# Twelve weight slots for the experts instead of six, and the upper and lower output rows of narrow experts in one tile

## What is computed

```python
combine = jnp.einsum('tk,tke->te', w, jax.nn.one_hot(eidx, N_EXPERTS, dtype=jnp.float32))
hid = jax.nn.silu(jnp.einsum('td,edf->tef', t, w_gate)) * jnp.einsum('td,edf->tef', t, w_up)
hid = hid * combine.astype(hid.dtype)[..., None]
return jnp.einsum('tef,efd->td', hid, w_down).reshape(B, L, D)
```

## Time and profile before

| | us |
|---|---|
| median of 3 runs | 1324.78 |
| lowest and highest | 1319.63, 1330.17 |
| the profiled execution | 1327.07 |
| its span, first to last instruction | 1325.4 |
| PE busy in the span | 1187.1 (90%) |
| DVE, ACT busy | 702.0 (53%), 433.7 (33%) |
| chain that ended last, its shares | PE 69%, DMA 15%, DVE 8% |
| expert stage of layer 0 | 379.2 to 645 |
| expert stage of layer 1 | 1018.0 to 1289 |

### The profile page before, as it was taken

The page is one execution under the profiler, slowest core; times in us unless marked ns, Lnnn a source line. Parts: engine busy times, 40 slices in busy tenths (PEclk is TensorE's granted clock), DMA queues, the critical chain, the costliest instruction groups (busy, mean ns, idle before and its releaser), DMA issues.

```text
span 1325.4 us, 20656 instructions
## 1 busy us (share of the span) xinstructions
PE 1187.1 (90%) x6340; PEld 755.7 (57%) x6341; DVE 702.0 (53%) x1425; ACT 433.7 (33%) x771; POOL 9.8 (1%) x30
## 2 busy tenths in 40 slices
PE   5999999998579999999689999999958899999973
PEld 2796555588354455444369755557926454455443
DVE  4365877664722344444566387767464234244445
ACT  2425555442331122222152345544233222122213
POOL 1000000000000000000000000000000000000000
PEclk8899999999699999999799999999978999999996
DMA  8743655423146899999783265552320889889961
GB/s 312 227 130 123 227 190 177 142 66 127 38 158 228 317 387 422 422 421 422 273 285 108 87 221 182 174 187 66 127 69 27 307 348 423 322 320 423 422 260 48
DMA packets 101983, 305.36 MB, mean 230 GB/s; under 512 B 7136, under 2 KB 47824, under 8 KB 77328
## 3 DMA queue, kind: packets, MB, share of 16 engines
q1 hardware_dynamic: 99248, 301.62, 61.0%
q10 hardware_dynamic: 2528, 2.50, 0.6%
q0 software_dynamic: 128, 0.26, 0.1%
HBM read 302.53 MB, written 1.84 MB: 230 GB/s over the span
## 4 chain that ended last, share of the span: by engine, by line
PE 69%; DMA 15%; DVE 8%; issue 4%; ACT 4%; DVEq 0%; SPq 0%; ACTq 0%
PE ps L694 14%; DMA ring<-in_w_e_up 13%; PE ps L557 9%; PE ps L589 6%; PE ps L560 6%; PE ps L680 5%; PE ps L715 4%; PE ps L716 3%; PE ps L717 3%; PE ps L612 3%; PE ps L878 3%; PE ps L641 2%; PE ps L653 2%; PE ps L785 2%; PE ps L760 1%
## 5 line engine op out<-in xcount | busy, mean ns | idle before, releaser
L557 PE MATMUL ps<-ring,xgT 128*64 128x256 f32 x1728 | 205.7, 387 | 16.5 <-issue 10.6
L557 PEld LDWEIGHTS ps<-ring,xgT 128*64 128x64 f32 x1728 | 125.9, 138 | 103.1 <-issue 27.7
L1420 DVE SCALAR_TENSOR_TENSOR nat<-ps,qT,nat 128x512 f32<-128x512 f32 x192 | 132.8, 745 | 80.6 <-PE ps L612 80.6
L694 PE MATMUL ps<-hT,ring 128*128 128x384 f32 x512 | 173.4, 492 | 0.0
L589 PE MATMUL ps<-ring,conv 128*64 128x512 f32 (+1 forms) x512 | 134.2, 597 | 7.2 <-issue 4.1
L1527 DVE SCALAR_TENSOR_TENSOR conv<-ub,dw,conv 128x414 f32<-128x414 f32 x240 | 136.6, 644 | 0.0
L694 PEld LDWEIGHTS ps<-hT,ring 128*128 128x128 f32 x512 | 95.4, 191 | 66.4 <-issue 7.2
L1411 DVE TENSOR_TENSOR orow_lo<-ps,orow_hi 64x512 fp32r<-64x512 f32 (+1 forms) x64 | 44.1, 689 | 112.5 <-ACT orow_hi L1037 111.7
L589 PEld LDWEIGHTS ps<-ring,conv 128*64 128x64 f32 (+1 forms) x512 | 48.3, 145 | 78.5 <-issue 78.2
L1402 DVE TENSOR_TENSOR csq<-csq,ps 128x256 f32<-128x256 f32 (+1 forms) x32 | 14.8, 463 | 129.4 <-PE ps L557 83.8
L560 PE MATMUL ps<-ring,xgT 128*128 128x512 f32 x160 | 74.8, 624 | 8.4 <-issue 8.4
(11 more groups left out here) (254 smaller groups left out, 1797.3 us busy)
## 6 DMA issues: line engine op xcount, KB each, us to landing
ring<-in_w_e_gate SPq DMA_DIRECT2D x64, 1024.0 KB, 10.1
ring<-in_w_e_up SPq DMA_DIRECT2D x64, 1024.0 KB, 10.8
ring<-in_w_e_down SPq DMA_DIRECT2D x64, 1024.0 KB, 9.8
ring<-in_w_ada SPq DMA_DIRECT2D x48, 1024.0 KB, 7.7
ring<-in_w_in SPq DMA_DIRECT2D x30, 1024.0 KB, 6.1
ring<-in_w_out SPq DMA_DIRECT2D x8, 1024.0 KB, 5.9
ring<-in_w_attn_proj SPq DMA_DIRECT2D x4, 1024.0 KB, 5.6
ring<-in_w_conv_proj SPq DMA_DIRECT2D x4, 1024.0 KB, 6.6
```

Source lines behind the costliest of these rows:

```text
L557: last = pe.matmul(ps[64 * hh:64 * hh + 64, b, 0:256], xgT[:, k, 0:64], ring[s][:, o + hh * 256:o + (hh + 1) * 256], start=(k == 0), stop= ...
L694: last = pe.matmul(ps[:, b, 0:T], ring[c % SLOTS][:, o:o + P], rhs(k), start=(k == 0), stop=(k == k_tiles - 1))
L1420: dve.scalar_tensor_tensor(sums, ps[:, b, :], weight[:, t, bass.ds(at, 1)], sums, ALU.mult, ALU.add).then_inc(fr[b], 1)
```

## The change

- Six more slots of 1 MB, `odd0` to `odd5`, lie over tiles that the experts don't need (`sig` and what follows it, `probs`, `hT`, `qkv`). Experts with an even number use `ring`, those with an odd number `odd`; the semaphores are `landed` and `landed_odd`. `hid`, `silu`, `hidT`, `own` and `xgT` move to other places.
- Expert 1's loads are issued between expert 0's, each once its place is free: the slots over `probs` and `sig` during the mixer's output stage, the one after the second norm, the last two (down) when `spread` is done. From expert 2 on, a slot waits for the expert two ahead.
- PE's program now has the first expert, the second expert (four branches) and a loop over pairs, whose body has two experts of four branches each. Counted in the program's order, with a float32 matmul as its four records, the first expert is about 330 instructions in both; the loop body was about 815, the second expert is about 775, and the new loop body about 1,580.
- A narrow expert's remainders go to the other 64 partitions of `orow_hi`, so `back` has two matmuls of 128 rows for each token tile instead of four of 64. Wide experts are as before.
- The counts of the start (`START`) grow from 3 to 8, with the waits that refer to them.

```diff
-SLOT_USES = (NCHUNKS + MOE_CHUNKS * NE) // SLOTS
+SLOT_USES = NCHUNKS // SLOTS + NE // 2
...
-START = 3
+START = 8
...
-        hid = flat(csq, 0, DE)
-        silu = flat(csq, DE, 2 * DE)
-        hidT = flat(conv, 0, DE).rearrange("p (k n) -> p k n", k=KE)
-        own = flat(conv, DE, DE + NT * P).rearrange("p (t n) -> p t n", t=NT)
+        hid = over("hid", "qkv", 0, [P, DE], F32)
+        silu = over("silu", "qkv", DE, [P, DE], F32)
+        hidT = over("hidT", "qkv", 3 * D + NT * P, [P, KE, P], F32)
+        own = over("own", "hT", NT * ROWS, [P, NT, P], F32)
...
-        xgT = over("xgT", "probs", 0, [P, KD, P], F32)
+        xgT = over("xgT", "qT", 2 * NT * BLOCKS * NE, [P, KD, P], F32)
+        assert start_of["kT"] >= start_of["qT"] + 4 * (2 * NT * BLOCKS * NE + KD * P)
+
+
+        odd = [over("odd0", "sig", 0, [P, SLOT], F32), over("odd1", "sig", SLOT, [P, SLOT], F32),
+               over("odd2", "probs", 0, [P, SLOT], F32), over("odd3", "probs", SLOT, [P, SLOT], F32),
+               over("odd4", "hT", 0, [P, SLOT], F32), over("odd5", "qkv", 3 * D + NT * P + DE, [P, SLOT], F32)]
...
+        landed_odd = [sem(f"landed_odd{s}") for s in range(SLOTS)]
...
-                for j in range(MOE_CHUNKS):
+                    load(ring[s], landed[s], src)
+
+                def first_even(j):
                     wait_chunk_used(NCHUNKS - SLOTS + j, l)
-                    load(j, landed[j], expert_chunk(j, l * NE))
-
-                def reload(e, first=False):
+                    load(ring[j], landed[j], expert_chunk(j, l * NE))
+
+                def first_odd(j):
+                    if j == 2:
+                        b, n = use("pv", UNITS - 1, l)
+                        sp.wait_ge(full[b], n + 1)
+                    elif j < 2:
+                        b, n = use("cproj", KD - 1, l)
+                        sp.wait_ge(full[b], n + 1)
+                    elif j == 3:
+                        sp.wait_ge(xn_r, l * (2 * KD) + 2 * KD)
+                    else:
+                        b, n = use("spread", 2 * KD - 1, l)
+                        sp.wait_ge(full[b], n + 1)
+                    load(odd[j], landed_odd[j], expert_chunk(j, l * NE + 1))
+
+                first_odd(2)
+                first_even(0)
+                first_odd(0)
+                first_odd(1)
+                for j in range(1, 5):
+                    first_even(j)
+                first_odd(3)
+                first_even(5)
+                first_odd(4)
+                first_odd(5)
+
+                def reload(e, before_e, tiles, landed_s, first=False):
+
                     for j in range(MOE_CHUNKS):
                         if j in (0, 2, 4):
-                            sp.wait_ge(half, l * HALF_PER + e * 3 + (12 + START - 3 + {0: 1, 2: 2, 4: 3}[j]))
+                            sp.wait_ge(half, l * HALF_PER + before_e * 3 + (12 + START + {0: 1, 2: 2, 4: 3}[j]))
                         elif j in (1, 3):
                             b = {1: 2, 3: 3}[j]
-                            sp.wait_ge(full[b], lead(b, l, e - 1, first) + 1)
+                            sp.wait_ge(full[b], lead(b, l, before_e, first) + 1)
                         else:
-                            sp.wait_ge(full[6], l * PER[6] + e + (INIT[6] + MOE_AT[6]))
-                        load(j, landed[j], expert_chunk(j, l * NE + e))
-
-                reload(1, True)
-                with sp.Fori(2, NE) as e:
-                    reload(e)
+                            sp.wait_ge(full[6], l * PER[6] + before_e + (INIT[6] + MOE_AT[6] + 1))
+                        load(tiles[j], landed_s[j], expert_chunk(j, l * NE + e))
...
+                reload(2, 0, ring, landed, True)
+                reload(3, 1, odd, landed_odd)
+                with sp.Fori(2, NE // 2) as i:
+                    reload(i * 2, i * 2 - 2, ring, landed)
+                    reload(i * 2 + 1, i * 2 - 1, odd, landed_odd)
...
-                for rows, first in ((orow_hi, True), (orow_lo, False)):
+
+                parts = (orow_hi,) if small else (orow_hi, orow_lo)
+                for rows in parts:
                     for h in range(2):
                         b = h if t < 2 else 2 + h
-                        a, z, o = (64 * h, 64 * h + 64, 0) if small else (0, P, 512 * h)
-                        last = pe.matmul(ps[:, b, :], ownT[a:z, t * P:(t + 1) * P], rows[a:z, o:o + 512], start=first, stop=not first)
-                        if not first:
+                        last = pe.matmul(ps[:, b, :], ownT[:, t * P:(t + 1) * P], rows[:, 512 * h:512 * h + 512],
+                                         start=rows is parts[0], stop=rows is parts[-1])
+                        if rows is parts[-1]:
...
-                def expert(e, before_e=None):
+                def expert(e, pair, odd_one, before_e=None):
                     alone = before_e is None
+                    if odd_one:
+                        tiles, landed_s, land_at = odd, landed_odd, l * (16 * NE // 2) + (pair * 16 + 16)
+                    else:
+                        tiles, landed_s, land_at = ring, landed, l * (16 * SLOT_USES) + (pair * 16 + 16 * (NCHUNKS // SLOTS + 1))
...
-                expert(0)
-                with pe.Fori(0, NE - 1) as e:
-                    expert(e + 1, e)
+                expert(0, 0, False)
+                expert(1, 0, True, 0)
+                with pe.Fori(1, NE // 2) as i:
+                    expert(i * 2, i, False, i * 2 - 1)
+                    expert(i * 2 + 1, i, True, i * 2)
...
-                    a, z, o = (64 * h, 64 * h + 64, 0) if small else (0, P, 512 * h)
-                    act.activation(orow_hi[a:z, o:o + 512], ps[a:z, 5 + h, :], ACT.Copy).then_inc(hi_s, 1)
+                    a, z = (64 * h, 64 * h + 64) if small else (0, P)
+                    act.activation(orow_hi[a:z, 512 * h:512 * h + 512], ps[a:z, 5 + h, :], ACT.Copy).then_inc(hi_s, 1)
...
-                    a, z, o = (64 * h, 64 * h + 64, 0) if small else (0, P, 512 * h)
-                    dve.tensor_tensor(orow_lo[a:z, o:o + 512], ps[a:z, 5 + h, :], orow_hi[a:z, o:o + 512].bitcast(F32),
-                                      ALU.subtract).then_inc(fr[5 + h], 1)
+                    a, z = (64 * h, 64 * h + 64) if small else (0, P)
+                    at_h = slice(512 * h, 512 * h + 512)
+                    lower = orow_hi[64 - 64 * h:P - 64 * h, at_h] if small else orow_lo[:, at_h]
+                    dve.tensor_tensor(lower, ps[a:z, 5 + h, :], orow_hi[a:z, at_h].bitcast(F32), ALU.subtract).then_inc(fr[5 + h], 1)
 
```

More of the change, by code:

```diff
@@ L160, in build @@
         csq = sb("csq", [P, KC, CO])
+        gap = sb("gap", [P, 16])
         mix = sb("mix", [P, 2 * KD * T + 4 * T])
@@ L424, in wait_chunk_used, with load @@
                     sp.wait_ge(full[b], n + 1)
-            def load(slot, landed_sem, src):
+            def load(tile, landed_sem, src):
                 n = src.shape[-1]
                 k = src.shape[-2]
-                dst = ring[slot][:, 0:k * n].rearrange("p (k n) -> p k n", k=k)
+                dst = tile[:, 0:k * n].rearrange("p (k n) -> p k n", k=k)
                 sp.dma_start(dst, src).then_inc(landed_sem, 16)
@@ L448, in _ @@
                         if c in (0, 2, 4):
-                            sp.wait_ge(half, l * HALF_PER + {0: START - 2, 2: START - 1, 4: START}[c])
+                            sp.wait_ge(half, l * HALF_PER + {0: START - 5, 2: START - 4, 4: START - 3}[c])
                         else:
                             b = {1: 2, 3: 3, 5: 6}[c]
-                            sp.wait_ge(full[b], l * PER[b] + INIT[b] - (2 if c in (1, 3) else 0))
+                            sp.wait_ge(full[b], l * PER[b] + INIT[b] - (4 if c in (1, 3) else 1))
                     else:
@@ L504, in _ @@
                                     sp.wait_ge(full_o[b], l * (OSTEPS * back_to) + q * (NE * back_to) + e * back_to + 1)
-                                load(j, landed_o[j], expert_chunk(j, l * NE + e))
+                                load(ring[j], landed_o[j], expert_chunk(j, l * NE + e))
                     sp.wait_ge(full_o[6], l * OSTEPS + (OSTEPS + 1))
@@ L544, in _, with expert_parts @@
             pe.wait_ge(freed[7], INIT[7])
-            def expert_parts(n_of, lead_of, fr, fs, landed_s, land_at, half_s, own_s, own_at, xg_s, xg_at):
+            def expert_parts(n_of, lead_of, fr, fs, tiles, landed_s, land_at, half_s, own_s, own_at, xg_s, xg_at):
                 def products(which, b, small):
@@ L557, in products @@
                                 last = pe.matmul(ps[64 * hh:64 * hh + 64, b, 0:256], xgT[:, k, 0:64],
-                                                 ring[s][:, o + hh * 256:o + (hh + 1) * 256], start=(k == 0), stop=(k == KD - 1))
+                                                 tiles[s][:, o + hh * 256:o + (hh + 1) * 256], start=(k == 0), stop=(k == KD - 1))
                         else:
```

(14 more changed lines are left out.)

5 lines of the change are left out of this document (3 added, 2 removed).

## The result

| | before | after |
|---|---|---|
| median, 20 runs each, us | 1323.41 | 1331.80 |
| lowest and highest | 1316.86, 1330.17 | 1325.72, 1339.77 |
| the profiled execution | 1327.07 | 1332.29 |
| its span | 1325.4 | 1330.7 |

The ratio is 1.0065, with a 95% interval of 1.0049 to 1.0082. The change costs 0.65%: clearly above nothing, and less than the 1% that I had named as the border.

A forecast was written before the change was run, and what follows sets the result against it. Bounds: late narrow experts waiting for loads, and PE stalling on first visits to code. From 1327.1 us, less 23.6 gained, plus 36.9 of stalls and slow clock: 1340 profiled, 1338 median; range 1302 to 1354.

The forecast's parts named there:

- the likeliest case: Whole kernel: gains outweighed by new code stalls and slow clock, median 1338 us, range 1318 to 1352; chance 60%.
- slots: Late narrow experts stop waiting for loads: 11.0 us gained in layer 0, 5.8 in layer 1, 16.8 in all.
- one tile: Narrow experts' sums: two 128-row matmuls replace four of 64, saving 0.27 us an expert, 6.8 us for 25.
- three new stalls: PE's first branches before layer 0's expert 3 and layer 1's 3 and 4: 11.5, 10.3, 9.1 us, sum 30.9.
- slow clock behind them: The product after each new stall runs at a lower clock: 1.7 to 2.3 us each, 6 us in all.
- the two old stalls: Layer 0's expert 0 to 1 (5.97 us) and layer 1's 1 to 2 (5.26 us) would stall as before.
- rows 4: Profile rows of the wide case before, where two 128-row matmuls take 0.58 and 0.56 us; basis of the tile's saving.
- the second block: Code block fetched right behind a first at each new stall: 5.9 us, upper value taken; lower value nothing.
- That the stalls would be hidden: Rival: PE's stalls are not code, or are hidden; new boundaries under 3 us each, 1301 us; chance 20%.
- That the loop wouldn't stay: Rival: PE's new loop is fetched again, some 22 narrow boundaries paying 5.3 us or more: 1418 or 1540 us; 12%.
- That the feed stays the limit: Rival: loads still limit layer 0's late experts, the slots change nothing, stalls partly absorbed: 1325 to 1335 us; 8%.

The follow-up runs named there:

- the lean program: The changed kernel with PE's branch on the width of the expert before only around the three sums, not the whole expert: 1298.93 us, ratio 0.9799.
- The runs with other programs: Kernel before with only PE's longer pair-loop program: 1352.14 us; changed kernel with the old four matmuls of 64 rows: 1337.64 us.
- the kernel with 512 unused instructions: The lean program with twelve slots, plus 512 never-run instructions between the two halves of its loop: 1317.24 us, ratio 0.9958.
- the loop of 11.7 blocks: The lean program with twelve slots, plus 256 never-run instructions after each of the first two products in both loop halves: 1589.13 us, ratio 1.2015.
- the leaner program alone: The kernel before (six slots, old sums) with the branch on the expert before only around each of the three sums: 1316.83 us, ratio 0.9944.

## Why the prediction was right or wrong

1338 was forecast for the median, 1331.8 came: 6.2 us less, inside the likeliest case's own range, 1318 to 1352. The mechanism, the places and the sign were right. That the number came so close is in part luck: the net cost is a small difference between a gain of 21 and a loss of 28 us, and the terms missed by 7.1, 3.9, 2.8 and 2.4 us in both directions. I gave "slower by over 1%" 0.43 and "within 1%" 0.39; the latter came, and the forecast had lain on the border. Term by term, in us, against the profiled execution's 1327.07:

| term | forecast | measured |
|---|---|---|
| slots | -16.8 | -17.3 (12.7 + 8.3, less the tile's 3.7) |
| one tile | -6.8 | -4.0 |
| three new stalls | +30.9 | +23.8 |
| slow clock behind them | +6.0 | +8.4 |
| the two old stalls | 0 | -3.9 |
| sum | +13.3 | +7.0, against +5.2 |

**The slots: right.** Experts 5 to 15 of layer 0 took 12.7 us less, against 11.0 and 11 times the tile's 0.16. For layer 1, take its loss and put back what isn't the slots': 13.4 us of new stalls and 6.0 of slow clock, less 1.9 and 1.5 at the old stall, are 16.0; its stage lost 7.7, so 8.3 were gained (the remainder of a subtraction, not a reading of its own), against 5.8 + 12 x 0.16 = 7.7: 12 experts of layer 1 have a narrow one before them. The kernel before also stands for 0.43 us ahead of expert 6 (`1119.18 0.43 issue`), and the changed one doesn't. There was no idle time on DMA `w_e_up`, and a loss by expert 1's earlier loads doesn't show. The experiment's 17.9 us for slots and tile in the lean program is near as well.

**The one tile: mechanism right, size wrong.** The period was to be 13.3 us and is 13.43, against 13.59: 0.16 us for an expert, not 0.27, 4.0 us in all for 25 of them. The step that failed took 0.57 us for a pair of 128-row matmuls from rows 4, where two pairs follow each other. A pair by itself takes 0.66, as the timeline of the changed kernel shows:

```profile
496.42 0.73 PE L652 MATMUL ps<-orow_hi,ownT 128*128 128x512 f32 x2
497.08 1.29 PE L596 MATMUL ps<-odd,xgT 128*64 128x256 f32 x9
```

That is exactly what four matmuls of 64 rows took the earlier trace rows. In the wide case the two pairs take 1.14 us together: 0.66 for the first and 0.48 more for the second. My mean of both hid a part that every group pays once. What is won lies elsewhere, at the third tile: from the first transpose to the down product 1205.72 - 1204.32 = 1.40 us, against 1088.23 - 1086.68 = 1.55 before:

```profile
1086.68 0.48 PE ps L568 x3
...
1088.23 3.65 PE ps L589 x16
```

The three transposes of `own` make all of it. They take 0.48 us here and 0.33 us in the changed kernel (L607). The kernel before has both values: 0.48 where sums of 64 rows stand in front of them, 0.33 where the sums of a wide expert do, of 128 rows (`435.71 0.33 PE ps L568 x3`). (It has 0.48 in the first expert of layer 0 too, which has no sums.) In the kernel with twelve slots and four matmuls of 64 rows, the chain has 0.48 for 26 experts. So the one tile pays by what follows its matmuls, not by the matmuls. Why the transposes take longer behind 64 rows isn't known.

**The new stalls: places right, the second block over-priced in layer 1.** Layer 0's 2 to 3 was forecast at 11.5 us and took 10.34. It was forecast as two blocks, and three packets stand in it, so that it came so near is in part luck. Layer 1's were forecast at 10.3 and 9.1 and took 6.37 and 7.06. The step that failed is "I take the upper value, since the second is known only once the first has run". The packets of layer 0 stand one behind the other, as it says. Those of layer 1 don't: there two packets start within 0.8 us. The rows at 1095.7 above show it, and so do those of 1072.9 to 1073.5:

```profile
q8 instruction: 2, 0.03, 37.1%
```

The runs with other programs have 11.2 us at the boundary 3 to 4, with the packets one behind the other, three of them. When two are asked for together, and whether that or the third packet makes the difference, is open: the cases may differ in where the block borders fall, and no run moved the borders alone. The prediction counted the blocks that are run; the kernel with 512 unused instructions shows that jumped-over blocks come in as well.

**The slow clock: right, under-priced.** The three first products are 2.4, 2.9 and 3.1 us over their usual time, where I had taken 2 each, from the mean clock of the two old places. Both new places in layer 1 follow a longer stop than the old one there.

**The old stalls: "as before" was slightly off.** They went from 5.97 to 5.29 and from 5.26 to 3.39 us, and behind the second the product took 3.67 us instead of 5.14. The measured terms add up to 1.8 us more than the profiled executions differ by: 0.8 of it is in the rest of the span, and 0.8 in layer 0's experts 0 to 4, where the terms make 11.9 and the chain has 11.1. That part is not placed.

**The rivals.** That the stalls would be hidden fell: each cost over 6 us, and 3 was the border. That the loop wouldn't stay fell in this kernel, and its price was real: the loop of 11.7 blocks costs 290 us. The prediction had 117 to 239 us for it. That the feed stays the limit fell: the period is PE's own to the last expert.

## What to carry to other kernels

A branch to code that PE hasn't met costs 3 to 6 us of its time here where one block comes in, 5 to 7 where two do and 10 to 12 where three do, and mostly the clock is slow for the product behind it. So before a loop is unrolled or a branch doubled, count the blocks of 256 instructions that its first lap meets, with those that it jumps over, and set that against the gain: here a gain of 21 us stood against 28 us of stalls and slow clock. Branch late, around what really differs, and the same change takes the kernel 2% under the one before, 0.6% of it from the leaner program alone.

In a trace such a stall is idle time "issue" at a branch, with packets in the queue of kind "instruction", on the first visit only. If later laps show packets too, the loop is too long to stay.

## What the runs showed of the hardware that was not expected

- PE keeps a loop of 6.2 blocks (1,578 instructions) without fetching; one of 11.7 blocks is fetched again in every lap: 199 packets instead of 44, and 290 us.
- Code that is jumped over is fetched too: 512 instructions that never run cost 4 packets (48 instead of 44) and 18.3 us in two layers.
- A fetch of code is slower while the kernel's own loads move. With the DMA engines' share at 0.70 around the second stall the stalls were 32.5 us, with 0.07 16.9.
- Two packets of code can be under way at once. One boundary costs 7.06 us where two start within 0.8 us, and 11.25 where three come one behind the other.
- Two 128-row matmuls of 512 columns take 0.66 us from start to start where they stand alone, as four of 64 rows do, and a further pair 0.48. Three transposes behind them take 0.33 us, behind the 64-row ones 0.48.
- The leaner program still has stalls of 2.99 and 3.29 us at places where the longer one had 5.29 and 10.34, with one packet in each. What the remaining 3 us are made of, no run took apart.
